# Two fused transformer blocks on one core: gate halves and turned queries on ACT, taps on valid columns, a running sum in pieces, and an earlier rotation of the queries

## The reference

```
proj = x @ w_in[l]                       # 2048 -> 7168
ca, cg, hq, hf, hi, hg, rq, rk, rv, rg = split(proj)
y_conv = conv_mixer(ca, cg, w_dw[l], b_dw[l], ...)      # 512 wide
y_hgrn = hgrn2_mixer(hq, hf, hi, hg, lower_bounds[l], ...)  # 6 heads of 128
y_ret  = retention_mixer(rq, rk, rv, rg, positions, ...)    # 6 heads of 128
h = concat([y_conv, y_hgrn, y_ret]) @ w_out[l]
x = layer_norm(ALPHA * x + h);  f = square(relu(x @ w_ff1[l]))
x = layer_norm(ALPHA * x + f @ w_ff2[l])
```

## Time and profile before

| | |
|---|---|
| median of 3 runs | 3481.93 us (3479.95 to 3484.95) |
| profiled execution, own time | 3486.19 us |
| its span in the profile | 3484.4 us |
| mean granted clock of TensorE | 0.992 |
| layer 0's mixers, PE's blocks 4 to 95 and the turn behind | 70.5 to 387.4 us |
| layer 1's mixers, likewise | 1243.6 to 1571.0 us |

### The profile page before, as it was taken

The page is one execution under the profiler, slowest core; times in us unless marked ns, Lnnn a source line. Parts: engine busy times, 40 slices in busy tenths (PEclk is TensorE's granted clock), DMA queues, the critical chain, the costliest instruction groups (busy, mean ns, idle before and its releaser), DMA issues.

```text
span 3484.4 us, 42756 instructions
## 1 busy us (share of the span) xinstructions
PE 3397.1 (97%) x15987; PEld 2831.8 (81%) x15987; DVE 2222.3 (64%) x2582; ACT 1586.0 (46%) x1958; POOL 352.4 (10%) x390
## 2 busy tenths in 40 slices
PE   8999999999999999989999999999999989999999
PEld 7788778888888787878788888888888879888877
DVE  6986566555555788855665656666446676655654
ACT  4544444444444446434444434344455643455553
POOL 0034001010101000340101010100000132000100
PEclk9999999999999999999999999999999999999999
DMA  7645566666666664446766676766655601565634
GB/s 238 181 140 163 181 199 219 200 211 200 212 199 212 190 194 151 145 151 193 245 210 208 203 207 203 207 196 208 186 178 176 205 6 56 188 189 169 179 118 163
DMA packets 333659, 633.83 MB, mean 182 GB/s; under 512 B 27545, under 2 KB 37785, under 8 KB 331819
## 3 DMA queue, kind: packets, MB, share of 16 engines
q1 hardware_dynamic: 313104, 595.93, 55.4%
q0 software_dynamic: 11168, 29.18, 2.7%
q10 hardware_dynamic: 9216, 6.30, 0.6%
HBM read 612.44 MB, written 2.10 MB: 176 GB/s over the span
## 4 chain that ended last, share of the span: by engine, by line
PE 85%; DVE 9%; ACT 3%; DMA 1%; POOL 1%; issue 1%; SPq 0%; DVEq 0%; ACTq 0%; POOLq 0%
PE ps_unit L279 26%; PE ps_unit L281 26%; PE ps_unit L280 26%; DVE sb_w_lo L262 3%; DVE sb_conv_y L1260 2%; PE ps_mix L2732 2%; PE ps_mix L1334 1%; DMA sb_raw<-in_w_in_dram 1%; ACT sb_w_hi L255 1%; PE ps_mix L708 0%; PE ps_mix L307 0%; DVE sb_x L438 0%; PE ps_mix L3129 0%; PE ps_mix L3109 0%; DMA sb_raw<-in_e_w_in_dram 0%
## 5 line engine op out<-in xcount | busy, mean ns | idle before, releaser
L262 DVE TENSOR_TENSOR sb_w_lo<-sb_raw,sb_w_hi 128x1024 fp32r<-128x1024 f32 x1120 | 1377.2, 1245 | 1001.4 <-ACT sb_w_hi L255 996.4
L255 ACT ACTIVATE sb_w_hi<-sb_raw 128x1024 fp32r<-128x1024 f32 x1120 | 1172.6, 1059 | 1456.9 <-DMA sb_raw<-in_w_ff_dram 532.3
L279 PE MATMUL ps_unit<-sb_w_hi,sb_a_hi 128*128 128x512 f32 x3456 | 1365.3, 395 | 16.0 <-DVE sb_a_lo L750 11.1
L281 PE MATMUL ps_unit<-sb_w_hi,sb_a_lo 128*128 128x512 f32 x3456 | 1351.6, 391 | 0.0
L280 PE MATMUL ps_unit<-sb_w_lo,sb_a_hi 128*128 128x512 f32 x3456 | 1350.7, 391 | 0.0
L279 PEld LDWEIGHTS ps_unit<-sb_w_hi,sb_a_hi 128*128 128x128 f32 x3456 | 652.8, 189 | 155.2 <-DVE sb_a_lo L750 12.7
L281 PEld LDWEIGHTS ps_unit<-sb_w_hi,sb_a_lo 128*128 128x128 f32 x3456 | 652.0, 189 | 137.6
L280 PEld LDWEIGHTS ps_unit<-sb_w_lo,sb_a_hi 128*128 128x128 f32 x3456 | 653.1, 189 | 132.2
L279 PE MATMUL ps_unit<-sb_w_hi,sb_f_hi 128*128 128x512 f32 x1024 | 399.3, 390 | 0.0
L281 PE MATMUL ps_unit<-sb_w_hi,sb_f_lo 128*128 128x512 f32 x1024 | 398.6, 389 | 0.0
L280 PE MATMUL ps_unit<-sb_w_lo,sb_f_hi 128*128 128x512 f32 x1024 | 398.5, 389 | 0.0
(11 more groups left out here) (463 smaller groups left out, 1975.6 us busy)
## 6 DMA issues: line engine op xcount, KB each, us to landing
sb_raw<-in_w_ff_dram SPq DMA_DIRECT2D x512, 512.0 KB, 3.8
sb_raw<-in_w_in_dram SPq DMA_DIRECT2D x224, 512.0 KB, 3.6
sb_raw<-in_e_w_in_dram SPq DMA_DIRECT2D x112, 512.0 KB, 3.5
sb_raw<-in_o_w_in_dram SPq DMA_DIRECT2D x112, 512.0 KB, 3.8
sb_raw<-in_w_out_dram SPq DMA_DIRECT2D x64, 512.0 KB, 3.7
sb_raw<-in_e_w_out_dram SPq DMA_DIRECT2D x32, 512.0 KB, 3.5
sb_raw<-in_o_w_out_dram SPq DMA_DIRECT2D x32, 512.0 KB, 3.5
sb_raw<-in_e_w_mem_kv_dram SPq DMA_DIRECT2D x16, 512.0 KB, 3.8
```

What stands on the lines that cost most here:

```text
L255: k.nc.scalar.activation(k.w_hi[:, j], k.raw[:, j], ACT.Copy).then_inc(k.hi_ready, 1)
L262: k.nc.vector.tensor_tensor(k.w_lo[:, j], k.raw[:, j], k.w_hi[:, j].bitcast(F32), ALU.subtract).then_inc(k.lo_ready, 1)
L279: k.nc.tensor.matmul(acc, hi[:, kt, tokens], w_hi, start=kt == 0, stop=False)
L281: last = k.nc.tensor.matmul(acc, lo[:, kt, tokens], w_hi, start=False, stop=kt == KT - 1)
```

## The change

The change has five parts, all in the first block.

1. ACT makes both halves of the gates from PSUM, Relu(-f) into `h_lf` and Relu(f) into `h_k`, behind the Ln; the two reads by DVE and the counter between the engines go. DVE's subtraction negates `h_lf` as well. It stands behind tap 27, and the step for `h_k` behind tap 28, each one tap later. Two more blocks stand between ACT's steps, and in layer 1 the small Ln follows the large one.
2. `conv_u` has no padding. The taps go from the latest to the earliest, and tap number `back` reads columns 0 to 256 - back and adds to columns back to 256. POOL's memset goes.
3. The two memsets and the scan of 1536 columns become 12 scans of 128 columns, each with the constant ones as its factor.
4. ACT copies the turned queries out of PSUM, at block 44 (48), and DVE waits for it.
5. POOL rotates the queries when 10 units are evicted, before the gate times the gain; the keys follow behind the gate, when 11 units are evicted as before.

```diff
@@ -1037,7 +1037,6 @@
 LEVELS = 7
 LOG_LB_MAX = math.log(1 - 1e-6)
 LOG_1M_LB_MIN = math.log(1e-6)
-CONV_T = CONV_W - 1 + SEQ
 CONV_TILES = CONV_C // P
 LATE = 4
 
@@ -1057,7 +1056,7 @@
     k.conv_rows = k.sb("conv_rows", t1, [CONV_W + 1, CONV_C])
     k.conv_gain = k.sb("conv_gain", t1 + 2 * K, [P, CONV_C])
     k.conv_shift = k.sb("conv_shift", t1 + 4 * K, [P, CONV_C])
-    k.conv_u = k.sb("conv_u", t1 + 6 * K, [P, CONV_C // P, CONV_T])
+    k.conv_u = k.sb("conv_u", t1 + 6 * K, [P, CONV_C // P, SEQ])
     k.conv_y = k.sb("conv_y", t1 + 11 * K, [P, CONV_C // P, SEQ])
     k.conv_w = k.sb("conv_w", t1 + 15 * K, [P, CONV_C // P, CONV_W + 1])
 
...
@@ -1181,7 +1180,6 @@
         pool.dma_start(k.h_gain[:], d["hgrn_norm_g"][l].partition_broadcast(P)).then_inc(*k.h_gain_in.up(16))
         if l:
             pool.dma_start(k.h_lb_rows[:], d["hgrn_lb"]).then_inc(*k.h_lb_in.up(16))
-    k.nc.gpsimd.memset(k.conv_u[:, :, 0:CONV_W - 1], 0.0).then_inc(*k.conv_pad.up())
     pool.wait_ge(*k.conv_gated.next("pool"))
     masks = d["c_levels"].rearrange("p (n t) -> p n t", n=LEVELS)
     for t, first, end in ((0, 0, 4), (1, 4, LEVELS)):
@@ -1245,22 +1243,22 @@
     dve.wait_ge(*k.conv_weights.next("dve"))
     v.tensor_copy(k.conv_w[:], k.ps[:, 0, 0:P].rearrange("p (c k) -> p c k", c=4)).then_inc(*k.dve_step.up())
     dve.wait_ge(*k.conv_turned.next("dve"))
-    v.tensor_copy(k.conv_u[:, :, CONV_W - 1:CONV_T],
+    v.tensor_copy(k.conv_u[:],
                   k.ps[:, 1:3, :].rearrange("p b (a s) -> p (b a) s", a=2)).then_inc(*k.dve_step.up())
-    dve.wait_ge(*k.conv_pad.next("dve"))
     dve.wait_ge(*k.dve_step.now())
     sem, done = k.conv_tap.now()
-    for tap in range(CONV_W):
+    for back in range(CONV_W):
+        tap = CONV_W - 1 - back
         for c in range(CONV_TILES):
-            u, y = k.conv_u[:, c, tap:tap + SEQ], k.conv_y[:, c, :]
-            if tap == 0:
-                ins = v.tensor_scalar(y, u, k.conv_w[:, c, 0:1], k.conv_w[:, c, CONV_W:CONV_W + 1], ALU.mult, ALU.add)
+            u, y, w = k.conv_u[:, c, 0:SEQ - back], k.conv_y[:, c, back:SEQ], k.conv_w[:, c, tap:tap + 1]
+            if back == 0:
+                ins = v.tensor_scalar(y, u, w, k.conv_w[:, c, CONV_W:CONV_W + 1], ALU.mult, ALU.add)
             else:
-                dve.wait_ge(sem, done + CONV_TILES * (tap - 1) + c + 1)
-                ins = v.scalar_tensor_tensor(y, u, k.conv_w[:, c, tap:tap + 1], y, ALU.mult, ALU.add)
+                dve.wait_ge(sem, done + CONV_TILES * (back - 1) + c + 1)
+                ins = v.scalar_tensor_tensor(y, u, w, y, ALU.mult, ALU.add)
             ins.then_inc(*k.conv_tap.up())
         run(1)
-        dve_hgrn_gates(dve, k, l, tap)
+        dve_hgrn_gates(dve, k, l, back)
     run(3 + LATE * l)
     dve.wait_ge(*k.conv_back.next("dve"))
     for t in range(TT):
@@ -1353,16 +1351,22 @@
         ins.then_inc(*k.act_step.up())
         act.wait_ge(*k.act_step.now())
 
-    act.wait_ge(*k.h_f_read.next("act"))
+    act.wait_ge(*k.h_fT.next("act"))
     step(a.activation(k.h_d1[:].rearrange("p (b s) -> p b s", b=3), k.ps[:, 0:3, :], ACT.Abs))
     run(1)
     step(a.activation(k.h_d1[:], k.h_d1[:], ACT.Exp, scale=-1.0))
-    a.activation(k.h_d1[:], k.h_d1[:], ACT.Ln, bias=1.0).then_inc(*k.h_softplus.up())
     if l:
         act.wait_ge(*k.h_lb_log.next("act"))
         step(a.activation(k.h_log[:, 3, :], k.h_log[:, 2, :], ACT.Abs))
         step(a.activation(k.h_log[:, 3, :], k.h_log[:, 3, :], ACT.Exp, scale=-1.0))
-        a.activation(k.h_log[:, 3, :], k.h_log[:, 3, :], ACT.Ln, bias=1.0).then_inc(*k.h_softplus.up())
+    run(1)
+    a.activation(k.h_d1[:], k.h_d1[:], ACT.Ln, bias=1.0)
+    if l:
+        a.activation(k.h_log[:, 3, :], k.h_log[:, 3, :], ACT.Ln, bias=1.0)
+    run(1)
+    a.activation(k.h_lf[:].rearrange("p (b s) -> p b s", b=3), k.ps[:, 0:3, :], ACT.Relu, scale=-1.0)
+    a.activation(k.h_k, k.ps[:, 0:3, :].rearrange("p b s -> p (b s)").rearrange("p (x n) -> p x n", x=2),
+                 ACT.Relu).then_inc(*k.h_softplus.up())
     upto(run, 34)
     act.wait_ge(*k.h_kx.next("act"))
     if l == 0:
@@ -1383,7 +1387,10 @@
     a = k.nc.scalar
     act.wait_ge(*run.evacuated(2))
     a.activation(k.h_q, k.h_q, ACT.Silu).then_inc(*k.h_qsilu.up())
-    upto(run, 43 + LATE * l)
+    upto(run, 44 + LATE * l)
+    act.wait_ge(*k.h_qT.next("act"))
+    a.activation(k.h_q, k.ps[:, 0:3, :].rearrange("p b s -> p (b s)").rearrange("p (x n) -> p x n", x=2),
+                 ACT.Copy).then_inc(*k.h_query.up())
     for level in range(LEVELS + 1):
         run(3)
         d = (k.h_d0, k.h_d1)[level % 2]
@@ -1440,25 +1447,18 @@
         ins.then_inc(*k.dve_step.up())
         dve.wait_ge(*k.dve_step.now())
 
-    f = k.ps[:, 0:3, :].rearrange("p b s -> p (b s)")
     log_lb, log_1m, delta, work = (k.h_log[:, n, :] for n in range(4))
     if tap == 22:
-        dve.wait_ge(*k.h_fT.next("dve"))
-        v.tensor_scalar(k.h_lf[:], f, 0.0, None, ALU.min)
-        v.tensor_scalar(k.h_k, f.rearrange("p (x n) -> p x n", x=2), 0.0, None, ALU.max).then_inc(*k.h_f_read.up())
         if l:
-
             dve.wait_ge(*k.h_lbT.next("dve"))
             step(v.tensor_copy(k.h_lb[:], k.ps[:, 3, 0:HEADS * DEPTH].rearrange("p (h n) -> p h n", h=HEADS)))
             v.tensor_tensor(delta, k.h_lb[:, :, 1], k.h_lb[:, :, 0], ALU.subtract).then_inc(*k.h_lb_log.up())
-    elif tap == 26:
-        dve.wait_ge(*k.h_f_read.now())
+    elif tap == 27:
         dve.wait_ge(*k.h_softplus.next("dve"))
-        step(v.tensor_tensor(k.h_lf[:], k.h_lf[:], k.h_d1[:], ALU.subtract))
-    elif tap == 27:
+        step(v.scalar_tensor_tensor(k.h_lf[:], k.h_lf[:], -1.0, k.h_d1[:], ALU.mult, ALU.subtract))
+    elif tap == 28:
         v.scalar_tensor_tensor(k.h_k, k.h_k, -1.0, in_halves(k.h_d1), ALU.mult, ALU.subtract).then_inc(*k.h_kx.up())
         if l:
-            dve.wait_ge(*k.h_softplus.next("dve"))
             v.scalar_tensor_tensor(log_lb, delta, 0.0, work, ALU.min, ALU.subtract)
             step(v.tensor_scalar(log_1m, delta, 0.0, -1.0, ALU.max, ALU.mult))
             step(v.tensor_tensor(log_1m, log_1m, work, ALU.subtract))
...
@@ -1491,14 +1490,12 @@
         step(last)
 
     dve.wait_ge(*k.h_kx.now())
-    v.memset(k.h_d0[:], 1.0).then_inc(*k.dve_step.up())
-    dve.wait_ge(*k.dve_step.now())
-    step(v.memset(k.h_d0[:].rearrange("p (n s) -> p n s", s=P)[:, :, 0:1], 0.0))
-    v.tensor_tensor_scan(k.h_cum[:], k.h_d0[:], k.h_lf[:], 0.0, ALU.mult, ALU.add).then_inc(*k.h_cumulated.up())
+    for n in range(TT * HEADS):
+        part = slice(n * P, (n + 1) * P)
+        last = v.tensor_tensor_scan(k.h_cum[:, part], k.ones, k.h_lf[:, part], 0.0, ALU.mult, ALU.add)
+    last.then_inc(*k.h_cumulated.up())
     upto(run, 44 + LATE * l)
-    dve.wait_ge(*k.h_qT.next("dve"))
-    v.tensor_copy(k.h_q, f.rearrange("p (x n) -> p x n", x=2)).then_inc(*k.h_query.up())
-    dve.wait_ge(*k.h_query.now())
+    dve.wait_ge(*k.h_query.next("dve"))
     dve.wait_ge(*k.h_key.next("dve"))
     dve.wait_ge(*k.h_mask_in.next("dve", 32))
 
@@ -1591,11 +1588,12 @@
 def pool_retention(pool, k, l):
 
     d = k.dram
-    pool_hgrn_gate(pool, k)
     pool.wait_ge(k.rotary.sem, 1)
-    pool.wait_ge(k.evacuated, 2 * BLOCKS + k.block0["pool"] + RV // NC * BLOCKS)
+    pool.wait_ge(k.evacuated, 2 * BLOCKS + k.block0["pool"] + (RK + NC - 1) // NC * BLOCKS)
     pool_rotate(pool, k, RQ)
     pool.sem_inc(*k.r_roped.up())
+    pool_hgrn_gate(pool, k)
+    pool.wait_ge(k.evacuated, 2 * BLOCKS + k.block0["pool"] + RV // NC * BLOCKS)
     pool_rotate(pool, k, RK)
     pool.sem_inc(*k.r_key_roped.up())
     pool.wait_ge(*k.r_rope_free.next("pool"))
...
```

11 lines of the change are left out of this document (5 added, 6 removed).

## The result

The changed kernel takes 3463.3 us in the median of five executions (3461.8 to 3464.3), the kernel before, run beside it, 3480.0 (3478.4 to 3485.0). The ratio is 0.9946, 95% interval 0.9935 to 0.9958: it is faster, by 16.6 us or 0.5%, and 3463 lies within the predicted 3448 to 3470. The profiled execution took 3461.8 us (span 3460.0), which is 24.4 less than the profiled execution before.

The account below looks back on a forecast made before the run. PE, busy 97%, was taken to bound the kernel, so only shorter PE waits and their clock losses count. Gains of 11.6 (layer 0) and 14.1 (layer 1) less 0.8 gave 25 us: 3457 from the median, range 3448 to 3470.

Parts of the forecast that it names:

- Gates and taps, 6.3 + 3.5 = 9.8: Tap stretch: PE's wait for the last tap in layer 0 (6.3 us) and for a split in layer 1 (3.5) shrink.
- The walk's moments: Layer 0 tap stretch, stepped through: last split waits about a microsecond for ACT, last tap ends 167.1, PE waits 1.3 us.
- rival 4: Taps writing at odd offsets: 0.2 us more per instruction makes the kernel slower, 3503 us; chance 0.03.
- Rotation: keys 3.9, r_rstd 1.4 + 3.8, key copy 2.7, less 0.8, together 11.0: Rotating queries early on POOL shortens waits for keys, HGRN scaling and ACT's key copy; 0.8 us lost beside DVE's factors.
- Running sum, 0: Twelve scans on DVE, 3.4 us better to 2.3 worse; hidden behind PE's other work, so worth 0.
- Turned queries, 4.1: Layer 1: ACT's copy removes PE's wait at L1500, 2.5 us, and 1.6 of clock.
- The 0.8 for levels 6 and 7: Cost in both layers of POOL's query rotation beside DVE's factors: 0.8 us, with 0 and 8 as ends.
- Rival 2: POOL beside the factors: PE waits 2.5 us with its clock at levels 6 or 7 per layer, 3465 us; chance 0.13.
- r_rstd, 0.4 left in each layer: PE's wait for DVE to finish HGRN: 1.4 of 1.8 us go in layer 0; layer 1 falls from 2.5 to 0.4.
- a surplus of 4.3: The profiled execution stood 4.3 us above the median of 3481.9, so the forecast went from 3461 to 3457.
- the three clock terms of 5.0: Lower clock behind PE's waits for POOL's keys (layer 0), a split and HGRN (layer 1): 1.6, 1.7 and 1.7 us.
- the 25: Whole predicted gain: layer 0 11.6 us, layer 1 14.1, less 0.8 for POOL beside DVE's factors.

Follow-up runs that it names:

- second profile of before: The kernel before with no edit, timed and profiled again beside itself: 3479.2 us, ratio 0.9999; its profiled execution took 3477.7.

## Why the prediction came out as it did

- **Gates and taps, 6.3 + 3.5 = 9.8.** Right in the sum: undone one at a time they cost 7.6 and 2.4, 10.0 together. Of the 9.8 the taps had only 0.8, in the first layer; how much of the measured 2.4 is theirs isn't shown. The walk's moments (1.04 us of waiting for ACT, last tap near 167.4) stand in the trace. The wait for the last tap is 1.8, not 1.3. The odd offsets cost nothing: all 240 taps lie between 444 and 479 ns, so rival 4 is out.
- **Rotation: keys 3.9, r_rstd 1.4 + 3.8, key copy 2.7, less 0.8, together 11.0.** Right in the sum, 11.3 when undone. Its terms aren't. With the old order the 2.3 for the keys came back without its clock (1.6), and the 2.7 for the key copy not at all (0.5). r_rstd grew to 3.9 us in the second layer, where the kernel before has 1.6 to 2.5. The copy tried alone in the kernel before points at the reason: with the wait for the query copy gone, PE comes sooner, and the wait for r_rstd reads 2.5 instead of 1.6. Waits that follow each other cover each other here, so that a later one looks smaller than it is once an earlier one has gone.
- **Running sum, 0.** Wrong in kind. Its own length came out as taken (3.90 us for twelve, estimated 4.1), but the memsets left unpriced were worth 1.4 us of VectorE's time, and behind the pieces VectorE's next splits were faster. Alone, undone, it shows 1.3; where the query copy is on VectorE, 6.3.
- **Turned queries, 4.1.** This is the step that failed. By the medians the price is right in the kernel before (3.5 alone). But the wait it was read from is also removed by the sum in pieces, so in this change the copy adds 0.
- **The place of ACT.** Missing from the sum. The diff line that puts ACT's unit work at 44 instead of 43 was read as part of the copy and priced at nothing; it costs 4.0 us, and the trace shows evictions with waits of 3.4 us that now stand ahead of two Exps. The 0.8 for levels 6 and 7 looked for trouble there, but from GpSimd. Rival 2 named the levels and a wait of 2.5, and its mechanism isn't the one: with GpSimd's work the same the waits go.
- **r_rstd, 0.4 left in each layer.** 1.1 and 1.7 are left. The scaling does take 1.83 us in the second layer, with GpSimd idle, as the prediction had it, so the rotation beside it was only part of the cause: the release stood too late in VectorE's queue. Given earlier, it takes both waits away (2.8 us in the trace, 1.6 in the medians).
- **From profile to median.** The gain by profiles, 24.4, is the 16.6 of the medians plus the 6.2 by which the profiled execution of before stood above its median and the 1.5 by which the changed one stood below its own. The prediction took a surplus of 4.3 off the level and left in the gain what made it. In the second profile of before the three clock terms of 5.0, the 2.7 for the key copy and 0.9 of r_rstd are absent, 8.6 us, while the query copy has 1.6 more of waiting and some 1.0 more of clock, and the splits 0.8, together 3.4. That 25 and 24.4 agree is therefore no proof of the terms.

Taking off the two steps that failed gives 25 - 4.1 (queries) - 4.0 (place) = 16.9, and 16.6 was measured. That closeness is luck: the 25 still holds the 5.2 us net (8.6 - 3.4) that the second profile of before doesn't have. The time came out 6.3 above 3457: 8.4 less was gained than the 25, and the median of before was 2.0 lower than the one I started from.

The sturdier account is that of the runs. Undone one by one, the parts come to 7.6 + 2.4 + 11.3 + 1.3 - 4.2 = 18.4 us, against the 16.6 of all together. I take the rest as the cover just described and the microsecond to which medians can be set side by side; no run separates the two.

## What to carry to other kernels

When a part moves an engine to another place in a row of units, count where its blocking instruction (here an eviction every eight blocks) falls among the others afterwards, and read how long it waits there: 3.4 us ahead of an Exp in the new place, 0.6 in the old one. The shift by one block cost as much as the copy was meant to bring. Price parts against each other as well as against the kernel before: two edits that remove one wait are worth it once. Before a profile's waits are summed, ask how its own execution stands to the median, and take a wait that hangs on a DMA's arrival (7.57 us in one profile, 4.00 in the next) at less than its face. The same holds for the clock lost behind a wait: the same 2.3 us were followed by 0.50 in one profile and by 1.00 in the next.
